# A transformer layer's MLP rewritten in two phases, its second product by Strassen's scheme on 2x2 blocks

## The reference, cut to what matters

```python
x = x + g1[:, None, :] * (mix_lat @ w_out[layer])
h = modulate(rms_norm(x, norm2_gain[layer]), sh2, sc2)
x = x + g2[:, None, :] * (jnp.square(jax.nn.relu(h @ w_ff1[layer])) @ w_ff2[layer])
return rms_norm(x, final_gain)
```

## Time and profile before

| | us |
|---|---|
| median of 3 runs (2693.42 to 2698.97) | 2697.36 |
| the profiled execution, its time | 2696.4 |
| its span, first to last instruction | 2694.6 |

### The profile page before, as it was taken

One profiled execution on the slowest core, in us unless ns is written; L12 is line 12 of the kernel. 1 busy time (PEld: TensorE's weight loads), 2 busy tenths in 40 slices (PEclk: granted clock), 3 DMA queues, 4 the chain that ended last, 5 costly groups with the idle time before them and its releaser, 6 DMA issues.

```text
span 2694.6 us, 33279 instructions
## 1 busy us (share of the span) xinstructions
PE 2558.6 (95%) x12256; PEld 2114.1 (78%) x12256; DVE 1238.3 (46%) x1498; ACT 725.7 (27%) x936; POOL 956.5 (35%) x402
## 2 busy tenths in 40 slices
PE   6999889999999999997999999999999999999997
PEld 3689777777777887786888878878878788788786
DVE  3356558887887325666323232323322323323324
ACT  4244222222222223224322212222222122231222
POOL 0100323232232443342444444444444444444442
PEclk9999999999999999998999999999999999999998
DMA  9944643344443442562232222222222223232222
GB/s 363 325 144 161 202 149 125 126 138 136 134 149 132 167 164 94 180 200 89 94 109 96 101 94 94 96 92 96 99 94 94 95 94 101 87 101 94 95 94 102
DMA packets 118722, 350.52 MB, mean 130 GB/s; under 512 B 10576, under 2 KB 10832, under 8 KB 116688
## 3 DMA queue, kind: packets, MB, share of 16 engines
q1 hardware_dynamic: 118176, 348.27, 37.8%
q10 hardware_dynamic: 432, 0.54, 0.1%
HBM read 344.57 MB, written 4.19 MB: 129 GB/s over the span
## 4 chain that ended last, share of the span: by engine, by line
PE 59%; issue 28%; POOL 10%; DVE 1%; DMA 1%; ACT 1%; POOLq 0%; SPq 0%; DVEq 0%; ACTq 0%
PE bank L1165 10%; PE bank L1164 10%; PE bank L1166 10%; POOL w_lo L335 10%; PE bank L1178 9%; PE bank L1179 9%; PE bank L1180 9%; PE bank L1126 1%; PE bank L1196 1%; PE bank L1197 1%; PE bank L1198 1%; DMA ada_w<-in_w_ada 1%; DVE x_res L1098 0%; ACT junk_in L388 0%; PE bank L1114 0%
## 5 line engine op out<-in xcount | busy, mean ns | idle before, releaser
L335 POOL TENSOR_TENSOR w_lo<-raw,w_hi 128x1024 fp32r<-128x1024 f32 x398 | 956.3, 2403 | 1712.9 <-ACT w_hi L363 1712.9
L363 ACT ACTIVATE w_hi<-raw 128x1024 fp32r<-128x1024 f32 x440 | 466.4, 1060 | 1705.1 <-PE bank L1166 907.3
L1165 PE MATMUL bank<-h_lo,w_hi 128*128 128x512 f32 x1696 | 666.1, 393 | 15.4 <-issue 15.4
L1164 PE MATMUL bank<-h_hi,w_hi 128*128 128x512 f32 x1696 | 676.2, 399 | 3.0 <-POOL w_lo L335 2.9
L1166 PE MATMUL bank<-h_hi,w_lo 128*128 128x512 f32 x1696 | 665.5, 392 | 0.0
L1178 PE MATMUL bank<-w_hi,hid_hi 128*128 128x512 f32 x1024 | 398.3, 389 | 0.0
L1179 PE MATMUL bank<-w_lo,hid_hi 128*128 128x512 f32 x1024 | 398.3, 389 | 0.0
L1180 PE MATMUL bank<-w_hi,hid_lo 128*128 128x512 f32 x1024 | 398.3, 389 | 0.0
L1166 PEld LDWEIGHTS bank<-h_hi,w_lo 128*128 128x128 f32 x1696 | 322.1, 190 | 85.0 <-issue 16.6
L1164 PEld LDWEIGHTS bank<-h_hi,w_hi 128*128 128x128 f32 x1696 | 322.5, 190 | 67.9 <-POOL w_lo L335 3.4
L1067 DVE TENSOR_TENSOR hid_sb<-relu_sb 128x512 f32<-128x512 f32 x64 | 159.4, 2490 | 470.2 <-ACT relu_sb L620 470.2
(11 more groups left out here) (203 smaller groups left out, 2176.4 us busy)
## 6 DMA issues: line engine op xcount, KB each, us to landing
raw<-in_w_stream SPq DMA_DIRECT2D x440, 512.0 KB, 3.5
ada_w<-in_w_ada SPq DMA_DIRECT2D x192, 512.0 KB, 4.9
x_tok<-in_x SPq DMA_DIRECT2D x4, 1024.0 KB, 10.0
x_res<-in_x SPq DMA_DIRECT2D x4, 1024.0 KB, 12.2
out<-x_res SPq DMA_DIRECT2D x4, 1024.0 KB, 4.0
ctx_tok<-in_ctx_x SPq DMA_DIRECT2D x2, 1024.0 KB, 15.8
fin_row<-in_final_row SPq DMA_DIRECT2D x1, 1024.0 KB, 5.4
ws<-in_ws_t SPq DMA_DIRECT2D x1, 512.0 KB, 4.3
```

The source lines that it names most:

```text
L335: pool.tensor_tensor(w_lo[:, r % 2], raw[:, r], w_hi[:, r % 2].bitcast(F32), ALU.subtract).then_inc(lo_done, 1)
L363: act.activation(w_hi[:, r % 2], raw[:, r], ACT.Copy).then_inc(hi_done, 1)
L1164: pe.matmul(dst, wh, hi[:, kt], start=(kt == 0), stop=False)
L1165: pe.matmul(dst, wh, lo[:, kt], start=False, stop=False)
```

## The change

**Phase 1.** The first product runs over 32 pairs of hidden tiles, 4 units each (the stream is reordered so that a pair holds tiles t and t+4 of a block). From the two squared tiles, each split into two halves of 256 tokens, VectorE makes the seven left-hand operands of Strassen's scheme (Winograd's form: three of them blocks as they are, four sums), ScalarE rounds them, VectorE subtracts, and SP writes high and low parts to DRAM (`hid_kept`). The residual stream goes to DRAM too (`x_kept`), and g2 as a row (`g2_kept`, which replaces `gate_row(1)`).

**Phase 2.** The second product runs over 16 groups: 8 blocks of the hidden dimension x 2 column parts n. In a group the weights are 2x2 blocks B of 512x512 each, 8 units. VectorE makes the right-hand sums in place (T3, T2, T4, T1), ScalarE the high halves, VectorE (no longer GpSimd) the low halves. Each of seven products takes 2 operand units of 12 matmuls: 2 tiles x 2 token tiles x 3. The products run in three chains of PSUM banks: x (products 0, 2, 4, 6) goes on accumulating over all four, y (product 1) and z (3, 5). After each product VectorE adds the chain's two banks as they stand to one quarter of `y` (`add_y`), so a chain's partial sums are read in mid-chain, and TensorE waits for that before it accumulates on. Eight `final` steps in and behind the last group gate, add the residual and scale, and two `last_norm` end it. The diff, cut to its core:

```diff
-UNITS = U_MLP + 32 * BLOCKS
+PAIRS = 4 * BLOCKS
+U_F2 = U_MLP + 4 * PAIRS
+GROUPS = 2 * BLOCKS
+UNITS = U_F2 + 8 * GROUPS
+A11, A12, S2, S3, S1, A22, S4, A21 = range(8)
+B12, B11, B21, B22 = 0, 2, 4, 6
+OPERAND = (B11, B21, B11, B12, B11, B21, B22)
+CHAIN = ("x", "y", "x", "z", "x", "z", "x")
+TARGET = ((0, 0), (0, 0), (1, 0), (1, 1), (1, 1), (1, 0), (0, 1))
...
+        half_r = work("half", 4, [P, 8, 2, SEQ // 2], F32R)
+        raw2 = work("raw2", 20, [P, 4, UNIT])
+        w2_hi = work("w2_hi", 36, [P, 2, UNIT], F32R)
+        w2_lo = work("w2_lo", 44, [P, 2, UNIT], F32R)
+        hid_r = work("hid", 52, [P, PRODUCTS, 4, 2, SEQ // 2], F32R)
+        hid_kept = nc.dram_tensor("hid_kept", [BLOCKS, 4, P, PRODUCTS, SEQ], F32).ap()
...
+            load_quad(0, 0, 4)
+            load_quad(1, 0, 4)
+            sp.wait_ge(x_res_ready, 16)
+            for t in range(TT):
+                sp.dma_start(x_kept[t * P:(t + 1) * P, :], x_res[:, t]).then_inc(x_stored, 16)
             sp.wait_ge(mod2_made, 16)
+            sp.dma_start(g2_kept.rearrange("(k p) -> p k", p=P), mod2[:, 3], allow_slow_non_contiguous=True).then_inc(g2_stored, 16)
+            with sp.Fori(2, 24) as k:
+                load_quad(k, 0, 3)
+                store_pair(k - 2)
+                load_quad(k, 3, 4)
...
+            def next_operand(g, o):
+
+                last_use = {B12: 6, B11: 8, B21: 10, B22: 12}[o - o % 2] + o % 2
+                sp.wait_ge(lo2_done, 14 * g + (last_use + 1))
+                load_operand(g + 1, o)
+
+            def next_hid(b, p):
+
+                sp.wait_ge(unit_used, 28 * b + (U_F2 + 14 + 2 * p + 2))
+                load_hid(b + 1, p)
+
+            def second_loads(b):
+
+                for p, units in ((0, ()), (1, (0, 1)), (2, (2, 3)), (3, (4, 5)), (4, (6, 7)), (5, ()), (6, ())):
+                    next_hid(b, p)
+                    for o in units:
+                        next_operand(2 * b + 1, o)
...
-            with pool.Fori(U_V // 4 + 1, UNITS // 4) as q:
+            with pool.Fori(U_V // 4 + 1, U_F2 // 4) as q:
...
+            def half_split(m):
+
+                act.wait_ge(half_step, 4 * m + 4)
+                act.activation(half_r[:, 0:7, 0], half[:, 0:7, 1], ACT.Copy).then_inc(half_hi, 1)
+
+            def pair_act(m, w):
+
+                hi_next(U_MLP, m, 0)
+                half_split(m - 1)
+                hi_next(U_MLP, m, 1)
+                relu(2 * m, w, 4 * m + (U_MLP + 2))
+                hi_next(U_MLP, m, 2)
+                hi_next(U_MLP, m, 3)
+                relu(2 * m + 1, w + 1, 4 * m + (U_MLP + 4))
+
+            def operand_hi(g, n, i):
+
+                act.wait_ge(unit_used, 14 * g + (U_F2 + i - 3))
...
+            def square(i, w, m):
+
+                dve.wait_ge(relu_made, i + 1)
+                if w == 0 and not (isinstance(m, int) and m == 0):
+                    dve.wait_ge(hid_stored, 16 * m)
...
+            def half_low(m):
+
+                dve.wait_ge(half_hi, m + 1)
+                dve.tensor_tensor(half_r[:, 0:7, 1], half[:, 0:7, 1], half[:, 0:7, 0], ALU.subtract).then_inc(half_ready, 1)
...
+            def operand_low(g, n, i):
+
+                dve.wait_ge(hi_done, 14 * g + (U_F2 + i + 1))
+                hi, lo = operand_w(n, i)
+                dve.tensor_tensor(lo, raw_of(OPERAND[i // 2] + i % 2), hi.bitcast(F32), ALU.subtract).then_inc(lo2_done, 1)
...
+            def add_y(g, n, p, first=False):
+
+                i, j = TARGET[p]
+                dst = tile_pair(y, n, i, j)
+                dve.wait_ge(unit_used, 14 * g + (U_F2 + 2 * p + 2))
+                if first and p in (0, 2, 3, 6):
+                    dve.tensor_copy(dst, chain_banks(n, p)[:]).then_inc(y_added, 1)
+                else:
+                    dve.wait_ge(y_added, 7 * g + p)
+                    dve.tensor_tensor(dst, chain_banks(n, p)[:], dst, ALU.add).then_inc(y_added, 1)
...
+            def group_dve(g, n, before=None, after=None, first=False, finals=()):
+
+                if before is not None:
+                    add_y(before, 1 - n, 6, first and n == 1)
+                operand_low(g, n, 3)
+                sum_t2(g, 1)
+                if first and n == 0:
+                    half_low(PAIRS - 1)
+                operand_low(g, n, 4)
+                sum_t4(g, 0)
+                add_y(g, n, 0, first)
+                operand_low(g, n, 5)
+                sum_t4(g, 1)
+                sum_t1(g, 0)
+                operand_low(g, n, 6)
+                add_y(g, n, 1, first)
+                operand_low(g, n, 7)
+                sum_t1(g, 1)
+                operand_low(g, n, 8)
+                add_y(g, n, 2, first)
+                if finals:
+                    final(finals[0])
...
+                operand_low(g, n, 13)
+                if after is not None:
+                    operand_low(after, 1 - n, 0)
+                add_y(g, n, 5, first)
+                if after is not None:
+                    operand_low(after, 1 - n, 1)
+                    sum_t3(after, 0)
+                    sum_t2(after, 0)
+                    operand_low(after, 1 - n, 2)
+                    sum_t3(after, 1)
...
+            group_dve(GROUPS - 1, 1, GROUPS - 2, None, False, (0, 1, 2))
+            for k in range(3, 7):
+                final(k)
+            last_norm(1)
+            add_y(GROUPS - 1, 1, 6)
+            final(7)
+            last_norm(0)
...
+            with pe.Fori(1, PAIRS // 2) as k:
+                pair_pe(2 * k, 0)
+                pair_pe(2 * k + 1, 2)
+
+            def group_pe(b, g, n):
+
+                for i in range(14):
+                    p, h = i // 2, i % 2
+                    banks = two_banks[{"x": (2, 1)[n], "y": 3, "z": 0}[CHAIN[p]]]
+                    pe.wait_ge(lo2_done, 14 * g + (i + 1))
+                    if h == 0:
+                        if n == 0:
+                            pe.wait_ge(hid_landed[p], 16 * b + 16)
+                        if p in (2, 4, 6):
+                            pe.wait_ge(y_added, 7 * g + (p - 1))
+                        elif p == 5:
+                            pe.wait_ge(y_added, 7 * g + 4)
...
+            with pe.Fori(1, BLOCKS) as b:
+                group_pe(b, 2 * b, 0)
+                group_pe(b, 2 * b + 1, 1)
```

More of the change, by code:

```diff
@@ new lines, in _ @@
+            for o in range(4):
+                load_operand(0, o)
+            store_pair(PAIRS - 2)
+            for o in range(4, 8):
+                sp.wait_ge(lo_done, U_F2 - 7 + o)
+                load_operand(0, o)
+            store_pair(PAIRS - 1)
+            for o in range(8):
+                next_operand(0, o)
+            sp.wait_ge(hid_stored, 16 * PAIRS)
+            sp.wait_ge(g2_stored, 16)
+            sp.dma_start(g2_row[:], g2_kept.partition_broadcast(P)).then_inc(rows_landed, 16)
@@ L325, in _ @@
+            sp.dma_start(fin_row[:], final_row.partition_broadcast(P)).then_inc(rows_landed, 16)
+            second_loads(0)
+            with sp.Fori(1, BLOCKS - 1) as b:
+                for o in range(8):
+                    next_operand(2 * b, o)
+                second_loads(b)
+            for o in range(8):
+                next_operand(GROUPS - 2, o)
             for t in range(TT):
-                sp.wait_ge(fin_ready, t + 1)
-                sp.dma_start(out[t * P:(t + 1) * P, :], x_res[:, t]).then_inc(stored, 16)
+                sp.dma_start(x_mid[:, t], x_kept[t * P:(t + 1) * P, :]).then_inc(rows_landed, 16)
@@ L328, in _ @@
+            for i, t in enumerate((2, 3, 0, 1)):
+                sp.wait_ge(norm_made, i + 1)
+                sp.dma_start(out[t * P:(t + 1) * P, :], y[:, t]).then_inc(stored, 16)
             sp.wait_ge(stored, 16 * TT)
@@ new lines, in _ @@
+            hi_next(U_MLP, 0, 2)
+            relu(0, 0, U_MLP + 3, True)
+            hi_next(U_MLP, 0, 3)
+            relu(1, 1, U_MLP + 4, True)
+            pair_act(1, 2)
+            with act.Fori(1, PAIRS // 2 - 1) as k:
+                pair_act(2 * k, 0)
+                pair_act(2 * k + 1, 2)
+            pair_act(PAIRS - 2, 0)
+            hi_next(U_MLP, PAIRS - 1, 0)
+            half_split(PAIRS - 2)
+            hi_next(U_MLP, PAIRS - 1, 1)
+            relu(2 * PAIRS - 2, 2, U_F2 - 2)
@@ new lines, in _ @@
+            for i in range(3):
+                operand_hi(0, 0, i)
+            relu(2 * PAIRS - 1, 3, U_F2)
+            operand_hi(0, 0, 3)
+            half_split(PAIRS - 1)
+            for i in range(4, 14):
+                operand_hi(0, 0, i)
+            for i in range(14):
+                operand_hi(1, 1, i)
+            with act.Fori(1, BLOCKS - 1) as b:
+                for n in range(2):
+                    for i in range(14):
+                        operand_hi(2 * b + n, n, i)
@@ L652, in _ @@
+            for i in range(14):
+                operand_hi(GROUPS - 2, 0, i)
+            for i in range(14):
+                operand_hi(GROUPS - 1, 1, i)
+                if i in (10, 12):
```

(33 more changed lines are left out.)

296 lines of the change are left out of this document (178 added, 118 removed).

## The result

After: 2601.95 us, median of four runs (2600.03 to 2606.39); before beside it: 2696.77. The ratio is 0.9652, interval 0.9640 to 0.9664. The forecast was 2606 in a range from 2597 to 2640. The profiled execution has a span of 2601.0 us and a time of 2603.13.

The account below looks back on a forecast made before the run. TensorE was taken as the bound. The old span summed as 2694.6 - 87.0 - 3.6 - 20.5 + 5 + 13 = 2601.5, 2603 with small waits; 2.8 us from span to median gave 2606 us, range 2597 to 2640.

Parts of the forecast that it names:

- 1, 384 matmuls fewer: Second product on TensorE: 2688 matmuls instead of 3072, at 0.2267 us each, -87.0 us.
- Part 2: Row of g2 through DRAM instead of 32 small TensorE matmuls, -3.6 us; its scattered store costs only if over 16 us.
- Part 3: TensorE's loops: six old jumps of 3.4 us go, new loops of 192 and 336 matmuls don't stall, -20.5 us.
- Part 4: Phase 1's 32 pairs of 21.8 us: the chain of squares, sums, copy, subtraction and store has slack, cost 0.
- Part 5: Phase 2's 16 groups of 38.1 us: VectorE needs 33.3 us with 2.7 us smallest margin, DMA fits, cost 0.
- Part 6: Seam between the phases: VectorE's queued work makes TensorE's unit 4 wait, +5 us, bounds 2 and 10.
- Part 7: Behind group 15: VectorE's finals, ScalarE's row copies and the store lengthen the end, +13 us, bounds 8 and 20.
- Rival (a): Phase 2's loop of 336 matmuls stalls at its jumps as the old one did: +20.5 us, 2626; chance 0.20.
- rival (c): Every backward jump of TensorE stalls, whatever the loop's size: 20 jumps, +68 us, 2674; chance 0.03.
- the stall point of 1.29 us an operation: Phase 2: if VectorE's operations stood 1.29 us or more apart, each group would stall.
- (b): VectorE late in phase 2: at 1.35 us an operation, +17 us, with seam and end 2623 to 2635; chance 0.17.
- (d): Slower than before: VectorE's two-SBUF-input operations stretched in phase 2, 58 us a group, +320 us; chance 0.05.

Follow-up runs that it names:

- experiment 1: The kernel before with TensorE's loop over the MLP's blocks written out, so without backward jumps there: 2674.32 us, ratio to before 0.9906.
- experiment 3: The kernel after with the last pair's square, sums and subtraction, half_split and last store moved later at the seam between the phases: 2597.05 us, ratio 0.9637.
- experiments 6 and 8: Kernel after with two useless 128x1024 VectorE operations per loop group: 2613.13 us; the same with both B22 loads issued ahead of product 4's activations: 2604.72 us.
- Experiment 7: The kernel after with four useless 128x1024 VectorE operations added to each of the loop's 12 groups: 2650.66 us, ratio 0.9825.
- experiment 4: The kernel after with another end: finals moved earlier, x_mid loaded before the last operands, one row scaling moved from ScalarE to VectorE: 2599.78 us, ratio 0.9643.

## Why the prediction was right

| step | forecast | measured |
|---|---|---|
| 1, 384 matmuls fewer | -87.0 | -87.0 (count and pitch) |
| 2, `gate_row(1)` | -3.6 | -3.5 (a distance of 3.72 for one of 0.23) |
| 3, loops of TensorE | -20.5 | -19.75 (experiment 1) |
| 4, phase 1 | 0 | 0 (676.2 us, no new wait) |
| 5, phase 2 | 0 | 0 in the kernel after |
| 6, seam | +5 (2 to 10) | +6.4 (experiment 3) |
| 7, end | +13 (8 to 20) | +13.0 (2.5 and 10.5) |

The terms up to the last matmul give -87.0 - 3.5 - 19.75 + 6.4 + 2.5 = -101.35; the stretch fell by 101.4. The 1 to 2 us that I had set down for small waits did not come, and the part ahead of the MLP was 2.7 us shorter by chance: 2601.0 for a forecast of 2603 in span, 2601.95 for 2606 in time.

**Parts 1 to 3** came as told in their times, with two slips that cost nothing. In Part 2 the scattered store took 18.6 us to land, over the 16 from which it "would begin to cost": SP issued it at 1266.12 and the next unit's load at 1278.31, while it was still under way, and TensorE got no new wait behind it. In Part 3 the heads' loop was counted as 256 matmuls; from one backward jump to the next the trace has 310, so 336 lay nearer to a size shown to be free than the forecast knew. Rival (a), stalls at the loop of 336, and rival (c), at every jump, are refuted by the kernel after itself and by the one of 672. The border is not known better than between 672 and 768, and only if the two loops' other code makes no difference.

**Part 4.** The walk of a pair was right to 0.2 us up to the store, and the store landed 1.6 us sooner than forecast. The pair that starts at 1606.26, its first matmul and then VectorE's operations:

```profile
1606.26 0.39 PE L1484 MATMUL banks<-h_hi,w_hi 128*128 128x512 f32 x1
...
1608.03 2.50 DVE L1250 TENSOR_TENSOR half<-relu_sb 128x512 f32<-128x512 f32 x1 [5.47 <-ACT relu_sb L742]
...
1614.66 2.74 DVE L1266 TENSOR_TENSOR half<-half 128x1792 fp32r<-128x1792 f32 x1 [2.54 <-ACT half L747]
1623.69 0.69 DVE L1250 TENSOR_TENSOR half<-relu_sb 128x512 f32<-128x512 f32 x1 [6.30 <-DMA hid_kept<-half]
```

The second square is done at 4.3 (forecast 4.4), the subtraction at 11.1 (11.3), and the store has landed at 17.4 (19): 1.75 MB took 6.1 us and not 7 to 8. The first square of the next pair waits for it, which the forecast had named, and `relu`'s four banks hide that.

**Part 5.** The sizes were right: 33.06 us of VectorE a group (33.3), 1.218 us a low half, no wait of TensorE. The walk was right where experiments 6 and 8 test it: two operations more fit, if nothing else is late. What was wrong is the sentence that B22 "would be 2 us late, inside the margin. Cost 0". The cost was 0, but the delay is taken out of the same margin that the order of VectorE needs, in every second group. I had weighed the two one by one and not together; up to 1.2 us of the 2.7 were gone in the kernel after, and its real margin was too small for two operations that the walk alone would have let in. By the same reasoning the stall point of 1.29 us an operation, given there, was too high; no run tests it.

**Part 6.** The forecast put the wait at the right unit with the right cause. It named the lower clock without a size: 3.7 us are the standing still, 2.7 the clock.

**Part 7.** Step by step from group 15's start (2532.1: the last matmul's end less 38.1 less 2.5 of delays): add 5 ends at 38.8 (forecast 38.8), the four finals at 53.4 (52.8), final 7 at 59.1 (59), the row scalings near 64 (64.3), the span at 68.9 (68.7).

**Rivals (b) and (d)** did not come. Experiment 7 shows what (b) could have cost: with an extra 4.5 us a group, 3.65 us for each of twelve groups, with the lateness of B22 in it. (d) was priced too high at +320, since I stretched all 29 operations; the seven that read banks aren't stretched.

## What to carry to other kernels

An engine that works in order and is 87% busy has as margin not the 13% but the smallest distance, along its order, between when it is done and when it is wanted; walk it, and take every late transfer out of the same margin. When a scheme with fewer products moves work to another engine, look at who works beside it: 14 subtractions a group on GpSimd next to all of VectorE's low halves and sums cost more (251 us) than the scheme wins (87). And look for the cheap part first: a fifth of this gain was the old loop's backward jump.

## What the runs showed of the hardware

- A loop of 768 matmuls an iteration had a gap of 2.6 to 3.35 us behind the fourth matmul of each iteration entered by a backward jump, 3.3 us lost a jump with the clock behind it; one of 672 did not, though its instruction queue brought six packets against three for one of 336.
- A stall of 3.5 us of TensorE was followed by 11 matmuls at 0.43 us (the level of 1.2 GHz), 2.7 us more, in the kernel after, and by 7 in that of experiment 4. Of the old loop's six gaps of 2.6 to 3.35 us two were followed by such matmuls (3.05 and 2.8 us) and four were not, the longest among them. Gaps of 1.0 and 1.7 us, in group 15, were not either: one start of 0.34 us behind each, then 0.23 again.
- VectorE's 128x1024 with two SBUF inputs took 1.22 us alone and, by the means of its groups, 2.07 to 2.24 with GpSimd at work; with one input from a bank 1.22 and 1.21.
- Loads of 512 KB had a median landing of 4.2 us over the whole kernel, and B22 behind 1 MB of other data on the same queue made its user wait up to 2.5 us in the kernel with two more operations; issued ahead of that load it was never waited for.
